# Projection weights 192 bytes further on in SBUF: a change of placement alone

## What is computed

```
h    = rmsnorm(x, norm_w)
proj = h @ w_in                      # 1024 x (1536 + 512 + 8 + 8 + 4*512 + 8 + 2048) columns
(gdn_qkv, gdn_z, gdn_b, gdn_a, fox_q, fox_k, fox_v, fox_z, fox_f, gate_logit) = split(proj)
y_a  = gated_deltanet(gdn_qkv, ...)          # 8 heads of 64, chunks of 64 tokens
y_b  = forgetting_attention(fox_q, ...)      # 8 heads of 64, causal softmax with decay
g_a, g_b = split(sigmoid(gate_logit + gate_b))
x    = x + (g_a * (y_a @ w_up_gdn) + g_b * (y_b @ w_up_fox)) @ w_out
out  = rmsnorm(x, final_norm_w)
```

## Time and profile before

| | |
|---|---|
| median of 3 runs | 943.96 us (942.51 to 944.45) |
| the profiled execution | 942.96 us |
| its span, first to last instruction | 941.2 us |
| PE matmul / weight load busy | 924.7 us (98%) / 703.7 us (75%) |
| DVE / ACT / POOL (GpSimd) busy | 610.6 us (65%) / 472.6 us (50%) / 19.8 us (2%) |
| mean busy share of the 16 DMA engines by slice | from under 10% to 90%, mean 111 GB/s |

### The profile page before, as it was taken

How to read it: one execution, slowest core, us unless ns; L and a number is a source line. 1 busy time by engine, 2 the same in 40 slices (tenths; PEclk the granted TensorE clock), 3 DMA queues, 4 the chain that set the end, 5 groups by cost and what they waited for, 6 DMA issues and landing times.

```text
span 941.2 us, 15988 instructions
## 1 busy us (share of the span) xinstructions
PE 924.7 (98%) x6413; PEld 703.7 (75%) x6413; DVE 610.6 (65%) x984; ACT 472.6 (50%) x846; POOL 19.8 (2%) x29
## 2 busy tenths in 40 slices
PE   7999999999999999999999999999999999999997
PEld 6778787888788876676766666666667888888886
DVE  7587568799999934454486786867863524247262
ACT  7556654632866625532656547466454543334132
POOL 1000002020000000000000000000000000000000
PEclk9999999999999999999999999999999999999999
DMA  7011451249323393322553325234124332223162
GB/s 251 24 49 45 113 166 45 69 170 209 92 91 112 113 262 87 102 75 90 135 187 92 112 101 169 90 111 126 34 69 167 93 98 66 79 112 112 24 207 83
DMA packets 114576, 104.35 MB, mean 111 GB/s; under 512 B 33144, under 2 KB 94720, under 8 KB 114120
## 3 DMA queue, kind: packets, MB, share of 16 engines
q1 hardware_dynamic: 103112, 80.53, 31.1%
q10 hardware_dynamic: 10240, 18.62, 5.4%
q0 software_dynamic: 1152, 4.19, 1.4%
HBM read 76.32 MB, written 27.00 MB: 110 GB/s over the span
## 4 chain that ended last, share of the span: by engine, by line
PE 45%; DVE 3%; ACT 1%; DMA 1%; issue 1%; SPq 0%; DVEq 0%; ACTq 0%
PE pj L2296 6%; PE pj L2298 5%; PE pj L2297 5%; PE pc L2429 4%; PE pa L2395 3%; PE pa L2364 1%; PE pj L2307 1%; PE pj L2309 1%; PE pj L2308 1%; PE pb L2455 1%; PE pj L2567 1%; PE pj L2566 1%; PE pj L2565 1%; PE pb L2444 1%; DVE pa L2028 1%; PE pa L2399 1%
## 5 line engine op out<-in xcount | busy, mean ns | idle before, releaser
L147 PE MATMUL pj<-h_hi,w_hi 128*128 128x512 f32 x504 | 203.8, 404 | 0.5 <-DVE w_lo L135 0.5
L148 PE MATMUL pj<-h_lo,w_hi 128*128 128x512 f32 x504 | 196.9, 391 | 0.0
L149 PE MATMUL pj<-h_hi,w_lo 128*128 128x512 f32 x504 | 196.6, 390 | 0.0
L147 PEld LDWEIGHTS pj<-h_hi,w_hi 128*128 128x128 f32 x504 | 94.5, 188 | 23.9 <-issue 1.1
L149 PEld LDWEIGHTS pj<-h_hi,w_lo 128*128 128x128 f32 x504 | 94.6, 188 | 20.4
L148 PEld LDWEIGHTS pj<-h_lo,w_hi 128*128 128x128 f32 x504 | 94.7, 188 | 17.9 <-issue 0.2
L2296 PE MATMUL pj<-h_hi,w_hi 128*128 128x512 f32 x248 | 101.4, 409 | 0.3 <-PEq L327 0.3
L2297 PE MATMUL pj<-h_lo,w_hi 128*128 128x512 f32 x248 | 96.9, 391 | 0.0
L2298 PE MATMUL pj<-h_hi,w_lo 128*128 128x512 f32 x248 | 96.8, 390 | 0.0
L2296 PEld LDWEIGHTS pj<-h_hi,w_hi 128*128 128x128 f32 x248 | 46.5, 188 | 19.6 <-issue 10.1
L601 ACT ACTIVATE xc<-pj 128x512 f32<-128x512 f32 x39 | 23.3, 597 | 72.4 <-PE pj L149 71.8
(11 more groups left out here) (377 smaller groups left out, 1869.5 us busy)
## 6 DMA issues: line engine op xcount, KB each, us to landing
w_raw<-in_w_in SPq DMA_DIRECT2D x48, 512.0 KB, 4.4
fox_scratch<-xc ACTq DMA_DIRECT2D x39, 256.0 KB, 2.7
qkv<-in_x SPq DMA_DIRECT2D x8, 512.0 KB, 5.8
fa<-rows_scratch POOLq DMA_DIRECT2D x8, 512.0 KB, 4.8
rv<-fr_scratch SPq DMA_DIRECT2D x16, 256.0 KB, 3.9
ma<-m_scratch SPq DMA_DIRECT2D x8, 512.0 KB, 3.9
rv<-in_w_out SPq DMA_DIRECT2D x8, 512.0 KB, 3.8
w_raw<-in_x SPq DMA_DIRECT2D x8, 512.0 KB, 4.4
```

The source lines that it names most:

```text
L147: nc.tensor.matmul(o, w_hi[:, slot, k], h_hi[:, k, cols], start=(k == 0), stop=False)
L148: nc.tensor.matmul(o, w_hi[:, slot, k], h_lo[:, k, cols], start=False, stop=False)
L149: last = nc.tensor.matmul(o, w_lo[:, slot, k], h_hi[:, k, cols], start=False, stop=(k == KT - 1))
```

## The change

`sel` and `vecs` are asked for between `h_lo` and `w_raw`. So `w_raw`, `w_hi`, `w_lo`, `ident`, `blk_ones` and `cst` lie 64 + 128 = 192 bytes further on; `onesr` and everything behind it stay where they were. Nothing else differs, and the lists of instructions of the five engines are row for row the same.

```
         h_hi = sb("h_hi", [P, KT, S], F32R)
         h_lo = sb("h_lo", [P, KT, S], F32R)
+        sel = sb("sel", [P, 32])
+        vecs = sb("vecs", [P, 16])
         w_raw = sb("w_raw", [P, 2, KT, P])
         w_hi = sb("w_hi", [P, 2, KT, P], F32R)
         w_lo = sb("w_lo", [P, 2, KT, P], F32R)
         ident = sb("ident", [P, P])
         blk_ones = sb("blk_ones", [P, P])
         cst = sb("cst", [P, P])
-        vecs = sb("vecs", [P, 16])
         eps_t = vecs[:, 0:1]
...
-        sel = sb("sel", [P, 32])
         onesr = sb("onesr", [P, 1], F32R)
```

## The result

The changed kernel takes 944.82 us in the median of 20 runs (944.32 to 946.52), the kernel before on the same chip 942.55 (20 runs, 941.39 to 944.45): 1.0025 times as long, with a 95% interval of 1.0018 to 1.0032. That is 2.3 us slower. Forecast was no change at 944.0, with a range of 941.0 to 949.0. The time lies inside the range and only 0.8 us above the forecast, but that is luck: the forecast stood on the median of three runs, 943.96, which 20 runs put at 942.55. Against 942.55, no change was missed by 2.3 us, on the side of the slower rival. The profiled executions stand 944.94 to 942.96 us, their spans 943.1 to 941.2.

What follows compares the result with a forecast made beforehand. TensorE was taken to bound the kernel, busy 924.7 of 941.2 us, over half at the pace of 2,256 projection matmuls. Five terms of 0 on the median 943.96 gave 944.0 us, range 941.0 to 949.0.

Steps and rivals of the forecast that it cites:

- the slower rival: Loads hinder streamed rows at the new distance over all 2,256 projection matmuls: +5.0 us, 949.0 us; chance 0.13.
- Term 1: Pace of the 2,256 projection matmuls, by distance of loaded weights and streamed rows: taken as 0, bounds -29.6 to +29.6 us.
- the faster rival: A collision present now in the projection matmuls goes: up to 29.6 us back, 914.4 us; a tenth, 941.0 us; chance 0.12.
- The rule of two read ports: TensorE reads moving rows and weight loads through independent ports, so no distance could matter: 0 for the matmul pace.
- Terms 2, 3 and 5: Weight loads (0 to +0.2 us), high/low split (0.4 us at most), small tiles' short matmuls and scalars: each taken as 0.
- Term 4: Transfers into the weights: taken as 0, bounds -1.1 us (PE's wait vanishes) to +4.8 us (ACT's wait handed on).

Runs made afterwards that it cites:

- the third experiment: sel and vecs put ahead of h_hi, against the kernel before: rows and weights all 192 bytes further on, distance as before; 943.23 us against 942.40, ratio 1.0010.
- the fifth: w_hi and w_lo right behind h_lo, w_raw alone behind sel and vecs, against the kernel before; 943.37 us against 942.51, ratio 1.0009.
- the sixth: sel and vecs between w_raw and w_hi, against the kernel before; w_raw unmoved, w_hi, w_lo 192 bytes past a multiple of 256 from h_hi; 945.17 us, ratio 1.0022.

## Why the forecast of no change was wrong by 2.3 us

**Term 1, the pace, failed.** Its reading of the pace was right (226.4 ns, of which 13.1 above the columns), and so was its question: whether the distance of loads and streamed rows counts. The step that failed is "I take 0, since the two distances that can be read agree within 0.1 ns". The two distances, 0 and 256 past a multiple of 512, are both multiples of 256, as the prediction itself says of all distances shown where it weighs the faster rival. By the runs the pace repeats after 256 bytes: past a multiple of 512, 0 and 256 are one and the same case (and so are 192 in the projection and 448 in the last product of the third experiment, 228.9 ns both), and after 64 or 128 bytes it doesn't. The agreement said nothing about a distance between. The new one costs 2.3 ns in even stretches, inside the bounds of -13.1 to +13.1 ns that the term had.

**The slower rival was right, its price twice too high.** It was named as streams that collide at the new distance, over all 2,256 matmuls, with the pace as its mark and 0.84 ns as its threshold. A slower pace at the new distance is what happened, shown by the third experiment (weights where the change has them, distance of before, old pace) and by the fifth and the sixth (the whole effect comes with the two loaded tiles). That it is the load that hinders the moving rows is not shown; the runs show only that the pace goes with the distance of the two. Its price of 5.0 us took 2.2 ns for all matmuls. The 2.2 came from seven steps behind small matmuls, between starts given to 10 ns, which leaves it open by more than 1 ns (with starts to 1 ns the same seven steps take 229.7 ns, 3.0 above the even pace), and that it is near the measured 2.3 is luck. Also, some 530 of the steps, from 340 to 720 us, ran off the even pace before already, and there the change cost nothing or gave 0.5 us back. So +2.4 us in all by the table, of which the median shows 2.3. The chances had 0.16 on slower and 0.72 on no change; by the rows alone a period could not be excluded, and the chances should have stood closer.

**The rule of two read ports.** By the Trainium skill, page "SBUF — State Buffer", section "Who interferes with whom", TensorE's two read ports are independent, and the term would be 0. The twelve kernels of the experiments differ from the one before in placement alone, and their pace goes from 226.5 to 234.4 ns. The measurement decides: here the pace of TensorE depends on the distance of loaded and streamed rows, and the term was not 0.

**Terms 2, 3 and 5 were right.** Loads stay at 188 ns, heads sum to 34.2 and 34.0 us, splits take 1,058 and 1,220 ns. That `tokq` and `state` load as fast, within 2 ns, from odd multiples of 64 and 32 was a true answer to the question of the start, and START fell; it was not the question that decided.

**Term 4 was right within what can be told.** The landing went from 4.4 to 4.7 us in the median, ACT's wait from 4.8 to 4.1 us; a second one of ACT, in the second part, which the prediction left out, went from 1.1 to 1.0 us. `w_raw` moved without `w_hi` and `w_lo` gives 1.0009, with an interval that touches no change.

**The faster rival fell:** the multiples of 256 are the good distances, not the bad ones.

## What to carry to other kernels

Where matmuls with a load of weights each run back to back, place loaded and streamed tiles at a distance that is a multiple of 256 bytes, and read the pace in the order in time. The mean of a load is the same 188 ns at every distance, within 1, and that of a matmul shows a longer step only in part: where the step grew by 6.7 ns (64 bytes), the means of the three products of the first part went from 404, 391 and 390 to 409, 396 and 395 ns. This is measured for the one form of matmul in the table below. A small tile that is put in or taken out ahead of such a pair can cost 1% of the kernel here, and an experiment that adds one must restore the distance, or it measures this. When two points agree, ask what they have in common before taking their value for a third.

## What the runs showed of the hardware that I had not expected

The pace of 128 x 512 float32r matmuls, each with its own load of 128 x 128 weights, by the distance of loaded from streamed tile past a multiple of 256 bytes (from 200 to 210 us, in the first part; sure to some 0.2 ns, so 233.3 and 233.5 are one value):

| distance, bytes | ns per matmul | ratio of times |
|---|---|---|
| 0 | 226.6 | 1 |
| 16 | 233.3, elsewhere 226.5 | 1.0064 |
| 32 | 233.3 | 1.0101 |
| 64 | 233.5 | 1.0109 |
| 96 | 234.4 | 1.0123 |
| 128 | 233.5, elsewhere 232.5 | 1.0090 |
| 160 | 233.3 | 1.0107 |
| 192 | 228.9 | 1.0025 |
| 224 | 233.3 | 1.0102 |
| 240 | 226.7, elsewhere 228.3 | 1.0008 |

It is no slope: 0 is good, the 16 bytes on either side of it are good in some stretches and not in others, 192 lies between, all others cost 6 to 8 ns. The loads' own rows are 188 ns throughout, within 1. Why it is so stays open: that the two reads meet in the memory is an explanation that fits a period of 256 bytes and a pace that goes with the distance and not with either address, but none of these runs looks into it. Also open are why 192 is better than its neighbours, and what chooses between the rhythms at 16, 128 and 240. Not tried were `w_hi` and `w_lo` at different distances, and other distances for the up-projections, which stay at their distance and at 226.7 ns in even stretches in all these kernels.
